# Group norm of a decoder block: variance of each head from 32-column matmuls into rows of PSUM, and inverse roots taken as rows

## The reference

```python
    _, o = lax.scan(step, state0, xs_scan)
    o = seq_first(o)
    mean = jnp.mean(o, axis=-1, keepdims=True)
    var = jnp.mean(jnp.square(o - mean), axis=-1, keepdims=True)
    o = ((o - mean) * lax.rsqrt(var + RWKV_GN_EPS)).reshape(B, S, RWKV_WIDTH) * ln_g + ln_b
    bonus = jnp.sum(r * k * r_k, axis=-1, keepdims=True) * v
    return (o + bonus.reshape(B, S, RWKV_WIDTH)) * g
...
        h = h + jnp.concatenate([o_att, o_rwkv], axis=-1) @ w_out[l]
```

## Time and profile before

| | us |
|---|---|
| median of 3 runs | 1583.03 |
| lowest and highest | 1581.36 and 1583.54 |
| the profiled execution | 1580.49 |
| its span, first to last instruction | 1578.8 |
| PE busy (matmul), DVE, ACT, POOL in the span | 1530.4, 1325.6, 1081.8, 633.5 |

### The profile page before, as it was taken

The page is one execution under the profiler, slowest core; times in us unless marked ns, Lnnn a source line. Parts: engine busy times, 40 slices in busy tenths (PEclk is TensorE's granted clock), DMA queues, the critical chain, the costliest instruction groups (busy, mean ns, idle before and its releaser), DMA issues.

```text
span 1578.8 us, 29423 instructions
## 1 busy us (share of the span) xinstructions
PE 1530.4 (97%) x10453; PEld 1262.1 (80%) x10453; DVE 1325.6 (84%) x1458; ACT 1081.8 (69%) x1316; POOL 633.5 (40%) x371
## 2 busy tenths in 40 slices
PE   7999988889999999999999999999999999999997
PEld 6877767886888788878888888888888888888884
DVE  4246455555699999999999999999999999999996
ACT  4245531103478888778888887888888788888874
POOL 7000312101032234355554665555455554546653
PEclk9999999999999999999999999999999999999999
DMA  7321110001599999999999999999999999999994
GB/s 236 100 68 41 40 41 3 4 4 68 214 357 396 385 393 376 390 367 393 387 384 383 390 393 390 391 383 380 380 389 391 394 393 382 385 376 395 395 385 144
DMA packets 81274, 464.33 MB, mean 294 GB/s; under 512 B 11642, under 2 KB 12854, under 8 KB 33072
## 3 DMA queue, kind: packets, MB, share of 16 engines
q1 hardware_dynamic: 71424, 438.68, 70.3%
q0 software_dynamic: 9104, 24.52, 7.0%
q10 hardware_dynamic: 672, 0.07, 0.0%
HBM read 449.16 MB, written 23.13 MB: 299 GB/s over the span
## 4 chain that ended last, share of the span: by engine, by line
PE 87%; DVE 9%; issue 1%; DMA 1%; ACT 1%; POOL 0%; POOLq 0%; DVEq 0%; ACTq 0%; SPq 0%
PE banks L380 71%; DVE expert_w_lo L320 5%; PE banks L1840 5%; PE banks L2103 1%; PE banks L1933 1%; PE banks L2100 1%; PE banks L2085 1%; PE banks L1917 1%; DMA expert_w_raw<-in_moe_w_gate_dram 1%; PE banks L2038 1%; PE banks L2112 0%; PE banks L2497 0%; PE banks L2363 0%; PE banks L2340 0%; PE banks L1960 0%
## 5 line engine op out<-in xcount | busy, mean ns | idle before, releaser
L320 DVE TENSOR_TENSOR expert_w_lo<-expert_w_raw,expert_w_hi 128x1024 fp32r<-128x1024 f32 x764 | 908.8, 1253 | 23.4 <-ACT expert_w_hi L315 23.1
L315 ACT ACTIVATE expert_w_hi<-expert_w_raw 128x1024 fp32r<-128x1024 f32 x764 | 745.6, 1054 | 16.0 <-DMA expert_w_raw<-in_moe_w_down_dram 13.4
L380 PE MATMUL banks<-expert_w_hi,x_block_T_hi 128*128 128x512 f32 x1008 | 395.7, 393 | 2.5 <-DVE expert_w_lo L320 2.4
L380 PE MATMUL banks<-expert_w_lo,x_block_T_hi 128*128 128x512 f32 x1008 | 392.8, 390 | 0.0
L380 PE MATMUL banks<-expert_w_hi,x_block_T_lo 128*128 128x512 f32 x1008 | 392.7, 390 | 0.0
L742 POOL COPY scatter_gates<-slot_gate 128x1 f32 x26 | 239.9, 9229 | 238.2 <-DMA y_sums<-y_block,scatter_rows 238.2
L380 PEld LDWEIGHTS banks<-expert_w_hi,x_block_T_hi 128*128 128x128 f32 x1008 | 189.4, 188 | 43.4 <-issue 2.8
L380 PEld LDWEIGHTS banks<-expert_w_lo,x_block_T_hi 128*128 128x128 f32 x1008 | 189.2, 188 | 39.6
L380 PEld LDWEIGHTS banks<-expert_w_hi,x_block_T_lo 128*128 128x128 f32 x1008 | 189.4, 188 | 38.4
L380 PE MATMUL banks<-expert_w_hi,h_block_T_hi 128*128 128x512 f32 x528 | 209.0, 396 | 1.2 <-DVE expert_w_lo L320 0.6
L380 PE MATMUL banks<-expert_w_lo,h_block_T_hi 128*128 128x512 f32 x528 | 206.1, 390 | 0.0
(11 more groups left out here) (397 smaller groups left out, 1980.1 us busy)
## 6 DMA issues: line engine op xcount, KB each, us to landing
expert_w_raw<-in_moe_w_up_dram SPq DMA_DIRECT2D x128, 1024.0 KB, 6.3
expert_w_raw<-in_moe_w_down_dram SPq DMA_DIRECT2D x128, 1024.0 KB, 8.9
expert_w_raw<-in_moe_w_gate_dram SPq DMA_DIRECT2D x126, 1024.0 KB, 9.1
w_raw<-in_w_in_dram SPq DMA_DIRECT2D x24, 512.0 KB, 3.8
residual<-in_x_dram SPq DMA_DIRECT2D x8, 512.0 KB, 5.1
w_raw<-in_w_out_dram SPq DMA_DIRECT2D x8, 512.0 KB, 3.3
staged_raw<-in_moe_w_gate_dram SPq DMA_DIRECT2D x2, 1024.0 KB, 5.8
y_sums<-residual SPq DMA_DIRECT2D x4, 512.0 KB, 7.4
```

What stands on the lines that cost most here:

```text
L315: act.activation(self.hi[:, k % self.nhl, 0:width], self.raw[:, slot, 0:width], ACT.Copy)\
L320: dve.tensor_tensor(self.lo[:, k % self.nhl, 0:width], self.raw[:, (k - self.staged) % self.nraw, 0:width], self.hi[:, k % self.nhl, 0:wid ...
L380: last = pe.matmul(o, lhs, rhs, start=start and t == 0, stop=stop and t == 2, skip_group_check=preset)
```

## The change

The squares become the moving operand. Four matmuls (one for each h) take `head_cols` as the stationary operand: 128 rows by 32 columns, of which column 0 is one for the first head's 64 rows, column 1 for the second's, the rest zero. Each writes its own 32 partitions of bank 4, so row 32h+j has the sum of head 2h+j for 512 tokens. DVE adds the epsilon over the whole 128x512 tile (`GV`), ACT takes its root (`GR`), and `inverse_root` runs on 128x512. No flip and no copy follow: the spread takes 32 rows for each h, at partitions 32h, with `head_rows` as the stationary operand. `GR` and the scratch `GT` are slices of `X2T`, which is written later. The sums move in front of `out_first(1)`, the spread in front of `out_first(3)`. `NR` and `NV` stay for the other norm, of the keys. POOL builds the two constants among its first ones.

```diff
+        head_cols = sb("head_columns", [P, 32])
+        head_rows = sb("head_rows", [P, P])
...
-        NRT1 = sb("gn_inverse_T", [8, 512], scope=o_scope)
+        GV = sb("gn_variance", [P, 512], scope=o_scope)
...
+        GR, GT = X2T[:, 0, :], X2T[:, 1, :]
...
             ch.link(pool.memset(eye_c[:, :], 0.0))
+            ch.link(pool.memset(head_cols[:, :], 0.0))
+            for j in range(2):
+                ch.link(pool.memset(head_cols[64 * j:64 * j + 64, j:j + 1], 1.0))
+            ch.link(pool.memset(head_rows[:, :], 0.0))
+            for h in range(HP):
+                r = slice(32 * h, 32 * h + 32)
+                keep(head_rows, head_rows[r, :].rearrange("p (j d) -> p j d", j=2), [[-1, 2], [0, HD]], 0, 1, ALU.not_equal, 1.0)
...
             mix_high(2)
             act.wait_ge(S("norm_in"), 2)
-            act.activation(NR[:, :], NV[:, :], ACT.Sqrt).then_inc(S("norm_root"), 1)
+            act.activation(GR, GV[:, :], ACT.Sqrt).then_inc(S("norm_root"), 1)
             mix_high(3)
-            norm_rows(1, 5)
...
             gated_bonus(0)
+            dve.wait_ge(S("norm_ps"), 2)
+            dve.tensor_scalar(GV[:, :], bank[4], 1.0 / HD, GN_EPS, ALU.mult, ALU.add).then_inc(S("norm_in"), 1)
             mix_low(2)
-            dve.wait_ge(S("norm_ps"), 2)
-            dve.tensor_scalar(NV[:, :], bank[4][:, 0:8 * TT], 1.0 / HD, GN_EPS, ALU.mult, ALU.add)\
-                .then_inc(S("norm_in"), 1)
-            gated_bonus(1)
             dve.wait_ge(S("norm_root"), 1)
-            inverse_root(NR[:, :], NV[:, :], NT[:, :])
+            inverse_root(GR, GV[:, :], GT)
             dve.sem_inc(S("norm_inv"), 1)
             mix_low(3)
-            gated_bonus(2)
-            gated_bonus(3)
+            for h in range(1, HP):
+                gated_bonus(h)
...
             out_first(0)
-            out_first(1)
             pe.wait_ge(S("gn_sq"), HP)
             pe.wait_ge(S("gn_centered"), HP)
-            norm_sums(U2, 4)
+            for h in range(HP):
+                last = pe.matmul(bank[4][32 * h:32 * h + 32, :], head_cols[:, :], U2[:, h, :], start=True, stop=True)
+            last.then_inc(S("norm_ps"), 1)
+            out_first(1)
             out_first(2)
-            norm_flip(1, 5)
+            pe.wait_ge(S("norm_inv"), 2)
+            for h in range(HP):
+                r = slice(32 * h, 32 * h + 32)
+                pe.matmul(bank[4 + h], head_rows[r, :], GR[r, :], start=True, stop=True).then_inc(S("norm_bc"), 1)
             out_first(3)
-            pe.wait_ge(S("normT_ok"), 2)
-            for h in range(HP):
-                norm_spread(1, h, 4 + h)
```

More of the change, by code:

```diff
@@ L951, in norm_rows @@
                 act.wait_ge(S("normT_ps"), n + 1)
-                act.activation((NRT0, NRT1)[n][:, :], bank[b][0:8, :], ACT.Copy).then_inc(S("normT_ok"), 1)
+                act.activation(NRT0[:, :], bank[b][0:8, :], ACT.Copy).then_inc(S("normT_ok"), 1)
             def decay_sigmoid(h):
@@ L1978, in norm_spread @@
                         pe.wait_ge(S("kk_ok"), h - 1)
-                pe.matmul(bank[b], sel_T[:, h * P:(h + 1) * P], (NRT0, NRT1)[n][:, :], start=True, stop=True)\
+                pe.matmul(bank[b], sel_T[:, h * P:(h + 1) * P], NRT0[:, :], start=True, stop=True)\
                     .then_inc(S("norm_bc"), 1)
```

## The result

The changed kernel takes 1586.23 us, the median of 21 runs (1582.71 to 1593.65); the kernel before takes 1583.15 on the same chip (21 runs, 1577.47 to 1590.28). The ratio is 1.0031, with a 95% interval from 1.0016 to 1.0045: slower by about 5 us by the ratio; the two medians lie 3.1 apart. I had forecast 1.65 us less. The profiled execution of the changed kernel took 1587.06 us, with a span of 1585.3, so 6.5 more than the span of before.

What follows compares the result with a forecast made beforehand. PE, holding 87% of the span, was taken as the bound, with DVE becoming the group norm's path. Group norm -3.6 and start +1.95 gave -1.65 us, from 1583.03 to 1581.4; range 1578.0 to 1585.5.

Steps and rivals of the forecast that it cites:

- The group norm: Mean matmuls to the end of the loop of 48: 3.6 us gained, the rest spent waiting for DVE.
- Sums: Four variance matmuls on column parts of PE's array work side by side: 1.2 us instead of 3.47.
- spread: Group norm's spread matmuls on four row parts of PE's array: 1.2 us instead of 4.61.
- reciprocal: DVE's reciprocal in the group norm's inverse root: 3.37 us for 512 columns, extended from 4, 8 and 32 columns.
- PE's waits: New group-norm waits for DVE: 2.1 us before the spread, then 1.6 and 1.2 for gn_normed.
- Column parts do not take turns: Answers a rival: column parts take turns, sums 3.8 us, gain only 1.7, time 1583.3; chance 0.15.
- The drain on a change of tiling mode: Rule against the change: switching tiling drains PE's array; the scores pair's 1.06 us was taken to leave room for little.
- the clock falling in a new wait: Rival: PE's clock falls in the group norm's new waits; hidden if before 385, else 1583.1 to 1584.4; chance 0.12.
- The start: POOL's new constants delay the first power and x_scaled at program start: cost 1.95 us.
- The rival in which the selects are dear: POOL's new selects at the start cost 0.7 us each or more; 1586.2 at 1.5 each, up to 1592.6; chance 0.09.
- the last sentence of the sum: Both changed places precede the experts, and PE has no later slack to swallow the 3.6 gain or 1.95 cost.
- a time outside the range: Sign: a time outside 1578.0 to 1585.5 would mean something unseen moved in the experts.

Runs made afterwards that it cites:

- later_and_pad: Changed kernel with the new constants built behind the four powers and 14 two-column matmuls ahead of PE's inverse-root wait; 1576.84 us, measured again 1577.79.
- sums_earlier: later_and_pad with the four variance sums in the middle of out_first(0), between its two token tiles; 1577.79 us, ratio 0.9965 to the kernel before.
- before_consts: Kernel before with only the new constants built on POOL at the start, read by nothing; 1584.79 us, ratio 1.0025.
- consts_later: Changed kernel with the two new constants built behind the four powers of -1/2 instead of ahead of them; 1584.17 us, ratio 1.0004.
- pe_pad: Changed kernel with 14 two-column matmuls added ahead of PE's wait for the inverse root, restoring PE's code length; 1580.75 us, ratio 0.9997.
- before_short: Kernel before with two of the 16 variance matmuls, so PE's program is 56 instructions shorter; 1585.41 us, ratio 1.0014.
- pad_7: Changed kernel with 7 two-column matmuls (28 instructions) before the wait for the inverse roots; 1584.82 us, one execution.
- start_pad: Changed kernel with 14 two-column matmuls at the very start of PE's program, none in the group norm; 1581.92 us, ratio 0.9997.

## Why the prediction was wrong

**The group norm: right.** I forecast a gain of 3.6, the trace has 3.86. Sums 1.04 (1.2 forecast), spread 1.14 (1.2), reciprocal 3.34 (3.37), PE's waits 1.59, 1.44 and 1.11 (2.1, 1.6, 1.2), full clock behind 387. The step from three shapes of 4, 8 and 32 columns to 512 held within 1%. Column parts do not take turns: that rival, 3.8 us for the sums, is out. The estimate of up to 1.6 for the sums, from the speedup of three column tiles in the Trainium skill (TensorE: Matmul & The Clock Gate, Part 3), was too high, 1.25 for the spread a little. The drain on a change of tiling mode that the Trainium skill names (TensorEngine Tiling, Tiling Modes, Key Properties) can be no more than what is inside the 1.04 and 1.14. The clock did not fall in the new waits of the changed kernel. In both profiles of `later_and_pad` and in `sums_earlier` it fell behind the padding, for 3.4 us from 383.1 to 385.3 us on, and the group norm still took 32.8 to 33.1: so early a fall hides behind DVE, as the rival had said.

**The start: right, somewhat small.** 1.95 forecast, 2.36 measured. The selects cost 0.40 each (0.38 summed), and the memsets of 32 columns and of one column 0.12 each, as summed. The power came at 8.73 for 8.5, and DVE read it at 9.34, 2.09 behind the 7.25 of before; the rest came on PE, whose first projection matmul was 2.36 later. The rival in which the selects are dear fell with them.

**The step that failed** is the last sentence of the sum: "Both places come before the experts, and PE goes on without a slack that could swallow either." I asked who could give time back, not who could take some. The sum put everything behind the group norm at nothing, as if the rest of the program stood still when PE's program got 56 instructions shorter. It didn't: the branch behind the expert loop went from 0.36 to 4.68 us, and with the clock behind it that is +5.8, more than either term. The four kernels with 56 or 28 instructions less show 4.7 to 6.4 us there, the ten other profiled executions, of nine kernels, 0.36. -3.86 + 2.36 + 5.8 is +4.3; the ratio of 1.0031 is 4.9.

**No rival named it.** The nearest was the clock falling in a new wait; it did fall, but at 1516 us, in a wait that no semaphore makes. The last sentence, that a time outside the range would mean something in the experts, pointed to the place and not to the cause. The profile of before could have told more: the branch's row was there, and the instruction packets were in its table of DMA queues, with a wait of 0.7 us behind one of them. But no row of before had a long branch, so its price could not have been read from it.

The Trainium skill has the rule (Runtime: NRT & Kernel Launch, Instruction fetch mechanics): code is refilled in blocks of 16 KiB, ahead and in sequence, and a taken branch whose target is not in the window waits for a DMA. The traces agree, in the packets of 16 KB, in the one that is fetched during the loop where the branch is short and missing where it is long, and in the 1.37 us from the landing to the end of the branch. I had not looked for a rule on code in a change of arithmetic.

**Left open:** why the step lies between 28 and 55 instructions, since no trace shows where a packet's code begins; the +2.0 in time mixing, which lies inside the 5 us by which executions with equal code there differ; and why the start's 2.4 us read as 4.0 to 4.4 in the times (`before_consts`; `consts_later` against the changed kernel; `later_and_pad` against `pe_pad`), each with 3 to 4 us of uncertainty.

## What to carry to other kernels

Count the instructions that a change takes from or adds to an engine with branches in its program, and look at the branches' own rows in both profiles; a jump that the profile of before shows short can get long by a change a thousand microseconds earlier, and a few idle instructions put it right. Before trusting a difference of some microseconds, make a control that has the same code length and none of the change. The instruction queue tells the two cases apart before the branch is reached: look whether it moves a packet while the loop runs. And padding has a price as well: put it where the engine waits longer than the padding takes, or it becomes the path.

## What the chip showed that I had not expected

- A taken branch on PE took 0.36 us in ten profiled executions and 4.68, 5.58, 6.42 and 4.68 us in four. It is not the transfer alone: in the four the 16 KB packet took 0.96 us, started 2.3 to 4.1 us into the branch, and PE went on 1.36 to 1.39 us after it had landed. The start of the packet makes the difference between 4.68 and 6.42.
- The idle time that it makes is 4.3 to 6.1 us. In the changed kernel 3.4 us at the 1.2 GHz level follow it; in `consts_later`, `before_short` and `pad_7` that level lasts 6.8 us and begins 1.2 to 3.0 us before PE goes on.
- The releaser that the profile names for such a wait is whatever semaphore came last; here it was DVE's low part of the weights in three of the four kernels, which in the kernel before was there 0.7 us behind the start of the branch, and nothing in `consts_later`. Only the branch's own row and the instruction queue show the cause.
- Four fp32 matmuls of 512 columns on four column parts of the array take 1.04 us together, on four row parts 1.14, where one took 0.955 (two in 1.91).
- A matmul with two moving columns still takes 0.23 us in the group norm (28 records in 3.18 us), and 0.44 at the start of `start_pad` (28 in 6.14). 56 PE instructions that only wait on a semaphore that is there ran from 3.0 to 9.0 us and held PE's first transpose until 9.22, 1.3 later than in `later_and_pad`.
